# A two-layer trunk with a product-key expert layer: prompt tile first, its expert slots beside the latent front

## The reference

```python
h = rmsnorm(x, g_attn_norm) * (1 + sc1) + sh1
cq, ckv, krope, zb, qc, kc, vc, gates = split(h @ w_in)
oa = attention over low-rank q / kv, 8 heads of 96          # mixer A
ob = gelu(zb)[:512] * (w_s applied per 128-token chunk)     # mixer B
oc = windowed attention, 8 query heads on 2 key heads of 64 # mixer C
x += g1 * ((s(g0)*(oa@w_o_a) + s(g1)*(ob@w_o_b) + s(g2)*(oc@w_o_c)) @ w_out)
h = rmsnorm(x, g_ffn_norm) * (1 + sc2) + sh2
q = h @ w_pq                                   # 8 heads, 2 halves of 128
top 16 of 128 keys in each half, then top 16 of the 256 sums -> 16 experts a head
x += g2 * sum_k gate_k * gelu(u_k . h) * v_k   # 8 x 16 = 128 experts a token
```

## Time and profile before

| | |
|---|---|
| median of 3 runs | 5146.21 us (5142.45 to 5149.38) |
| span of the profiled execution | 5145.4 us, 0.8 us under the median |
| TensorE busy | 3978.3 us (77%) |
| VectorE busy | 2905.9 us (56%) |
| ScalarE busy | 1635.7 us (32%) |
| GpSimd busy | 1556.1 us (30%) |
| bytes moved by DMA | 1640.19 MB, of which 1342.26 MB by the gathers; 319 GB/s over the span |
| mean granted TensorE clock | 0.853 of full speed |

### The profile page before, as it was taken

How to read it: one execution, slowest core, us unless ns; L and a number is a source line. 1 busy time by engine, 2 the same in 40 slices (tenths; PEclk the granted TensorE clock), 3 DMA queues, 4 the chain that set the end, 5 groups by cost and what they waited for, 6 DMA issues and landing times.

```text
span 5145.4 us, 62465 instructions
## 1 busy us (share of the span) xinstructions
PE 3978.3 (77%) x20366; PEld 1626.3 (32%) x20366; DVE 2905.9 (56%) x6315; ACT 1635.7 (32%) x4867; POOL 1556.1 (30%) x1453
## 2 busy tenths in 40 slices
PE   5988899778887666666679889997788887666666
PEld 3555653332223211111134556533322232111111
DVE  3543544675666676654445434446756667766544
ACT  0211542223333333333322115422233333333333
POOL 0210012233334444343312100132333344444432
PEclk8989999988999977666779899998889998677666
DMA  7126049899999999999941260498899999999998
GB/s 281 48 78 236 7 167 399 344 339 372 421 406 409 420 421 421 421 421 421 421 183 48 99 221 1 179 398 340 341 373 421 411 409 413 421 421 421 421 421 357
DMA packets 232449, 1640.19 MB, mean 319 GB/s; under 512 B 26688, under 2 KB 28864, under 8 KB 36800
## 3 DMA queue, kind: packets, MB, share of 16 engines
q0 software_dynamic: 184320, 1342.26, 63.8%
q1 hardware_dynamic: 47808, 293.94, 15.0%
HBM read 1632.82 MB, written 3.28 MB: 318 GB/s over the span
## 4 chain that ended last, share of the span: by engine, by line
PE 37%; DMA 35%; DVE 17%; issue 5%; ACT 4%; DVEq 2%; POOL 1%; SPq 0%; ACTq 0%; POOLq 0%
DMA arena<-in_experts,arena 30%; PE ps L751 12%; PE ps L985 8%; DVE sq L1455 6%; DMA front<-in_experts,arena 3%; PE ps L936 3%; PE ps L961 3%; DMA arena<-in_weights 2%; PE ps L888 2%; PE ps L949 2%; PE ps L913 2%; PE ps L900 1%; ACT arena L1122 1%; DVE arena L1185 1%; DVE negm L1346 1%
## 5 line engine op out<-in xcount | busy, mean ns | idle before, releaser
L985 PE MATMUL ps<-arena 64*64 64x512 f32 x9040 | 1569.3, 777 | 828.2 <-ACT arena L1122 813.5
L724 POOL DMA_INDIRECT arena<-in_experts,arena x1130 | 1261.1, 1116 | 2774.9 <-PE ps L985 1891.6
L1455 DVE CUSTOM_DVE_ANT_0 sq<-arena 128x1024 f32<-128x1024 f32 x1130 | 1386.1, 1227 | 909.4 <-DMA arena<-in_experts,arena 831.3
L985 PEld LDWEIGHTS ps<-arena 64*64 64x64 f32 x9040 | 312.8, 156 | 1923.1 <-issue 1900.5
L1116 ACT ACTIVATE arena<-arena 128x1 f32<-128x1 f32 x1280 | 258.4, 202 | 2073.9 <-DVE arena L1455 2058.2
L751 PE MATMUL ps<-arena 128*128 128x512 f32 (+3 forms) x1920 | 819.3, 574 | 21.9 <-DMA arena<-in_weights 20.0
L1122 ACT ACTIVATE arena<-ident,arena 128x128 f32<-128x128 f32 x1280 | 513.9, 402 | 91.8 <-issue 3.4
L751 PEld LDWEIGHTS ps<-arena 128*128 128x128 f32 x1920 | 360.3, 195 | 467.5 <-issue 427.0
L1118 ACT ACTIVATE arena<-arena 128x1 f32<-128x1 f32 x1280 | 376.7, 294 | 92.1 <-issue 5.2
L961 PE MATMUL ps<-arena 128*128 128x256 f32 (+1 forms) x1536 | 349.3, 372 | 6.3 <-issue 2.3
L961 PEld LDWEIGHTS ps<-arena 128*128 128x128 f32 x1536 | 251.7, 199 | 183.4 <-issue 150.5
(11 more groups left out here) (159 smaller groups left out, 3039.4 us busy)
## 6 DMA issues: line engine op xcount, KB each, us to landing
arena<-in_weights SPq DMA_DIRECT2D x242, 1024.0 KB
arena<-in_experts,arena POOLq DMA_INDIRECT x1130
arena<-mod_rows SPq DMA_DIRECT2D x24, 512.0 KB, 7.1
arena<-in_weights SPq DMA_DIRECT2D x8, 576.0 KB
arena<-in_keysT SPq DMA_DIRECT2D x4, 1024.0 KB, 12.9
arena<-in_g_norm SPq DMA_DIRECT2D x6, 512.0 KB, 9.4
arena<-in_weights SPq DMA_DIRECT2D x4, 768.0 KB
arena<-in_weights SPq DMA_DIRECT2D x6, 512.0 KB
```

The lines of the kernel that those rows point to most:

```text
L724: pool.indirect_dma_start(out=ring[BUF[n]], out_offset=None, in_=ins["experts"], in_offset=bass.IndirectOffsetOnAxis(ap=index(t)[:, slot:s ...
L985: last = MM(acc[h][to:to + 64, c * 512:(c + 1) * 512], diag[n % 4][lo:lo + 64, lo:lo + 64], ring[BUF[n]][lo:lo + 64, D + c * 512:D + (c + ...
L1455: V.tensor_tensor_reduce(out=sq[:], in0=ring[BUF[n]][:, 0:D], in1=h2_of_slot(n), scale=1.0, scalar=0.0, op0=ALU.mult, op1=ALU.add, accum_o ...
```

## The change

The list is written in another order. The prompt runs through inputs, attention, merge, route and choose alone. Its 128 slots are then spread through the whole front of the latent tiles (inputs, attention, merge and route of tile 1). The 512 latent slots follow, with merge and route of tile 2 and then of tiles 3 and 4 spread in, and in layer 0 also the modulation products and the whole prompt front of layer 1. There are now four groups for merge and route, and the input weights are loaded twice a layer (once for the prompt, once for the latents).

```diff
-GROUPS = {0: (0,), 1: (1, 2), 2: (3, 4)}
+GROUPS = {0: (0,), 1: (1,), 2: (2,), 3: (3, 4)}
...
+def prompt(l):
+    norms = first_norms(l, (0,))
...
+    s = norms + inputs_of(l, (0,)) + attention(l, (0,))
+    s += [("rows2", l, 0), ("keys", l, 0)] + merge(l, 0) + route(l, 0, 0)
+    return s
+
+def sample(l):
+    s = first_norms(l, SAMPLE) + inputs_of(l, SAMPLE) + attention(l, SAMPLE)
+    s += [("rows2", l, 1), ("again", l), ("keys", l, 1)] + merge(l, 1) + route(l, 1, 1)
+    return s
...
 def schedule():
-    s = [("start",), ("consts", 0)] + mod_items(0, (0, 1))
+    s = [("start",), ("consts", 0)] + mod_items(0, (0, 1)) + prompt(0) + [("g2", 0, 0)]
     for l in range(L):
...
-        s += attention(l, (1, 2, 3, 4), choose(l, 0)) + [("rows2", l, 1), ("keys", l, 1), ("g2", l, 0)]
         line = Line()
-        line.slots(l)
-        line.spread(-3, 118, pieces(merge(l, 1) + route(l, 1, 1)))
-        line.spread(140, 236, choose(l, 2))
-        line.spread(118, 320, pieces(merge(l, 2) + route(l, 2)))
-        line.spread(322, 372, choose(l, 3))
+        line.slots(l, (0,))
+        line.spread(-1, 134, pieces(sample(l)))
+        s += line.items() + [("g2", l, 1)]
+        line = Line()
+        line.slots(l, SAMPLE)
+        line.spread(-2, 96, pieces(merge(l, 2) + route(l, 2, 2)))
+        line.spread(96, 236, pieces(merge(l, 3) + route(l, 3, 3)))
+        line.spread(240, 300, choose(l, 4))
         if l == 0:
-            line.spread(400, 630, mod_items(1))
-        line.spread(390, 490, choose(l, 4))
+            line.spread(238, 320, [("consts", 1)] + mod_items(1))
+            line.spread(320, 500, pieces(prompt(1)))
```

```diff
-NBUF = 11
-RELEASE = {6: lambda l: ("pq", l, 1, 15), 7: lambda l: ("pq", l, 2, 15), 8: lambda l: ("o", l, NT - 1, 1),
-           9: lambda l: ("sc", l, 2, 15), 10: lambda l: ("n2", l, NT - 1)}
+NBUF = 9
+ALWAYS = 3
+RELEASE = {3: lambda l: ("sw", l, 0), 4: lambda l: ("om", l, NT - 1, 1), 5: lambda l: ("om", l, NT - 1, 1),
+           6: lambda l: ("pq", l, 2, 15), 7: lambda l: ("pq", l, 3, 15), 8: lambda l: ("tk1", l, 3, 15, 1)}
+RETIRE = {3: lambda l: ("hT1", l + 1, 0), 4: lambda l: ("Emm", SLOTS * NT * (l + 1) - 8), 5: lambda l: ("Emm", SLOTS * NT * (l + 1) - 8)}
...
-                elif item[0] == "qT" and item[2:] == (0, 0):
-
-                    l = item[1]
-                    for n in range(l * NT * SLOTS, (l + 1) * NT * SLOTS):
+                elif item[0] == "G":
+                    n = item[1]
...
-        acc = [ps[:, 2 * h:2 * h + 2, :].rearrange("p a n -> p (a n)") for h in range(2)]
+        acc = [ps[:, h, :] for h in range(2)]
...
-                            last = MM(acc[h][to:to + 64, c * 512:(c + 1) * 512], diag[n % 4][lo:lo + 64, lo:lo + 64],
+                            last = MM(acc[h][to:to + 64, :], diag[n % 4][lo:lo + 64, lo:lo + 64],
...
     elif _k == "O":
         if _it[4] == 1:
-            _take(_it, _it[3], 1)
+            _take(_it, 2 + _it[3], 1)
+            _open.add(2 + _it[3])
     elif _k in PAIR:
-        _take(_it, min((4, 6) if _open else (2, 4, 6), key=lambda b: max(_used[b:b + 2])), 2)
+        _take(_it, min((b for b in (2, 4, 6) if not _open & {b, b + 1}), key=lambda b: max(_used[b:b + 2])), 2)
     elif _k in ONE:
-        _take(_it, min(range(4, 8) if _open else range(2), key=lambda b: _used[b]), 1)
+        _take(_it, min((b for b in range(2, 8) if b not in _open), key=lambda b: _used[b]), 1)
```

More of the change, by code:

```diff
@@ L60 @@
 TILES = (0, 1, 2, 3, 4)
+SAMPLE = (1, 2, 3, 4)
 CTX = (5, 6)
@@ new lines @@
+GATHER_AFTER = {}
+_free = {b: -1 for b in range(ALWAYS)}
+_in = {b: (None, 0) for b in range(NBUF)}
+_at = -1
+for _n in range(NSLOT):
+    _l, _s = divmod(_n, NT * SLOTS)
+    _t = _s // SLOTS
+    if _s == 0:
+        for _b in RELEASE:
+            _free[_b] = AT[RELEASE[_b](_l)]
+    _ok = [b for b in _free if b not in RETIRE or AT[("Emm", _n)] < AT.get(RETIRE[b](_l), len(BASE))]
+    _b = min(_ok, key=lambda b: _free[b])
+    _at = max(_at, _free[_b], AT[("tk2", _l, _t, _s % SLOTS // 32, 5)])
+    assert _at < AT[("E", _n)], (_n, _b)
+    GATHER_AFTER.setdefault(_at, []).append(_n)
+    _free[_b] = AT[("Emm", _n)]
+    BUF.append(_b)
+    SAME[_n] = _in[_b][0]
+    TURN_OF[_n] = _in[_b][1] + 1
+    _in[_b] = (_n, TURN_OF[_n])
```

539 lines of the change are left out of this document (281 added, 258 removed).

## The result

The changed kernel took 5410.98 us as the median of 4 runs (5399.06 to 5419.69), the kernel before 5147.8 us on the same chip (5142.45 to 5152.48): a ratio of 1.0507, 95% interval 1.0494 to 1.052. The forecast was 5215 us, at most 5375. The direction was right, the loss four times as large as forecast (263 us against 67). The span of the profiled execution, 5397.2 us, is 181 us over the 5216 of the sum.

| stage | forecast | measured | off |
|---|---|---|---|
| A, prompt alone | 387 | 387.3 | 0 |
| B, layer 0: norms and inputs | 268 | 287.2 | +19 |
| latent attention (slots 48 to 97) | 330 | 360.8 | +31 |
| merge of tile 1 / route and choose | 120 / 114 | 130.0 / 112.7 | +10 / -1 |
| B, layer 1: the same four | 268, 330, 120, 114 | 288.1, 366.9, 130.5, 112.1 | +20, +37, +11, -2 |

The account below looks back on a forecast made before the run. It took TensorE to bound the fronts, DMA the slot stages from 7 buffers on, and VectorE to limit route with 6. Terms 387 + 832 + 1674 + 832 + 1491 = 5216 gave a forecast of 5215 us, range 5030 to 5375.

Parts of the forecast that it names:

- A: Prompt alone through inputs, attention, merge, route and choose, up to the first slot: 387 us.
- B: Prompt slots beside the latent front, once in each layer: 832 us each.
- D: The latent slots of layer 1: 1491 us.
- C: The 512 latent slots of layer 0, including the prompt front of layer 1: 1674 us.
- the term of the latent attention in B: 64 units with 47 slots: 17 units at 3.6 us, 47 at 5.5 us of ScalarE, plus 10: 330 us.
- the ring: Rival: first 97 prompt slots have three circulating buffers and stall if gathers land after over 8.4 us; 5375 to 5533, chance 0.12.
- The attention's own upper bound, 395: Latent attention in B if every slot's 3.64 us of ScalarE came on top in series: 395 us.
- Inputs: Latent norms and inputs in B, with 45 slots in the inputs and TensorE full there: 268 us.
- Merge: Merge of tile 1 in B with 17 slots, 110 us of DMA plus waits at its start: 120 us.
- The turn: The last 12 slots of C and the turn to the next layer: 26 us.
- The prompt front in C: 180 slots beside the prompt front of layer 1, counted by DMA bytes, its attention's table loads covered: 575 us.
- the attention hides it: Rival: table loads fall into TensorE's 207 us, so the latent attention takes 258 and B 760: 5071 us, chance 0.23.

Follow-up runs that it names:

- slot_tanh: The changed kernel with the slot's Gelu replaced by a Tanh, which shares a table set with the Exp: 5266.62 us (one run).
- no_slots_in_attention: The changed kernel with no slots beside the 64 units of latent attention; 43 prompt slots of a layer run later: 5522.93 us, ratio 1.073.
- late_with_free_pairs: Control (changed kernel, all prompt slots behind the latent attention, 5632.61 us) with the values' product moved to banks 0 and 1: 5432.39 us (one run each).
- freed_and_tanh: The changed kernel with no bank held through a mixer, and the Gelu of slots inside an attention made from Square, Tanh and Identity: 5165.48 us, ratio 1.003.

## Why the forecast was wrong

A was right to 1 us, and not by luck: the inputs ended near 150 us, the attention at 190 and the merge at 289, where its terms put 152, 192 and 290. D was right to 10, C's first three parts to 11. One of these holds a slip: 75 slots and 22 blocks are 242 us at 2.49, not 248, so slots 226 to 364 should have stood at 456, against 469 measured.

The step that failed is the term of the latent attention in B, the largest of the misses with 31 and 37 us: "17 units without a slot at 3.6, and 47 where ScalarE does Exp 1.09, copy 0.80 and 3.64". I had taken the tie of scores to the Exp just before as an addition to ScalarE's load, at 3.5 us a unit, which I read from one round of the kernel before at full clock, and let the slot's work and the loads stand in its place. They are two causes. The closed bank pair alone takes 280 us for 64 units, 4.4 a unit, since the round of 3.6 is joined by waits at the ends of mixers and the clock falls (0.84); the loads come on top with 60, and the slots' other work with 6 and 3 (slot_tanh against no_slots_in_attention). The table loads themselves, which I argued at length, were sized well: 94 x 1.3 = 122 us of ScalarE forecast, 119 measured for 89 loads, half of it on the path. In this order of the runs 286 + 6 + 60 is the measured 352 from the first to the last Exp; the stage by its slots is 9 longer. From the other end it is 254 us for the stage with neither cause, against the bound of 258 in the prediction, and 107 for the two, where the prediction had put 72 on top.

The count that should have warned was in my hands: 32 of 64 scores bound instead of 10. I let a tied unit cost 3.6 us against 207 / 64 = 3.2 of the stage before, 0.4 more; late_with_free_pairs against its control gives 93 / 64 = 1.45 over all units, tied or not. The count alone gives no price either, as the 21 bound scores of freed_and_tanh show: it matters what TensorE has to do in the meantime.

The upper end of the range, 5375, came from the ring alone, and the ring's bytes are worth 20 us in both layers together. The attention's own upper bound, 395, was wide enough (65 us a layer above 330, 5346 in the sum), but I left out that the other terms would lean the same way. Without the 68 us of the attention, or without the 58 of the end of C, the time would have been under 5375; it took both. Inputs +19 and +20: half the ring, the rest not tried apart. Merge +10 and +11: not tried. The turn +20: 2 found, the rest open. The prompt front in C +38: 15 a late row, and 17 the table loads, which I had called covered because 35 slots "give it 110 us". The row shows why a stretch that is bound by bytes doesn't cover such a wait: while VectorE stood for it no buffer came free, the stretch moved 381 GB/s instead of 420, and the bytes weren't made up later.

The rival *the attention hides it* would have needed both causes gone. freed_and_tanh has them gone, with 254 us for what it put at 258. It takes 5165 us and not the rival's 5071, since the misses in inputs, merge and C stay. So, as far as that kernel shows it, the trade of the change (idle DMA in the fronts against 88.6 MB of weights) came out at +0.3%, and its two side effects cost 4.8%. The direction was right because the attention holds up the change, on which the forecast rested too: without its 72 us a layer the sum is 5071.

## What to carry to other kernels

Before work is overlapped with a stage, count what it holds there, not only what it executes: here two accumulator banks, closed for the whole program, cost the attention 92 us and more a layer with no slot in it, and about 50 with 47 slots in it. Size a tie by running or reading the whole stage with it, since waits also lower the clock of the matmuls between them. Two functions of different table sets that are interleaved on ScalarE want a form of one in the set of the other, and only where they meet: in all slots the longer form took back most of what it gave. Batches of slots between batches of units were not tried.

## What the runs showed of the hardware

TensorE's granted clock changes level inside one attention. Two windows of the changed kernel, the first behind a wait of TensorE of 1.4 us (ended at 705 us), the second behind waits of 1.6 and 2.8 us (ended at 716 and 723 us). The granted clock was 1.00 from 698 to 725 us and 0.50 from there to 739:

```profile
706.00:712.00 6.00, 5.50 (x51) 3.69 (x50) 2.25 (x4) 4.92 (x8) 1.62 (x1) 1.00 0.28 75
726.00:733.00 7.00, 5.53 (x32) 3.08 (x31) 2.09 (x5) 5.15 (x9) 0.94 (x1) 0.50 0.35 116
```

At 1.00 (2.4 GHz) a slot's eight matmuls take 1.09 us, at 0.50 (1.2 GHz) 1.98. The 64 units of attention, the same instructions, are 178 us of TensorE at a mean of 0.98 and 219 at 0.84. And a table load of 1.28 us cost less than that in time, 0.7, on a ScalarE that is busy for three quarters of the stage. A part of the loads falls into waits: the one at 702.50 us above ends at 703.78, and the maximum for which its Exp waits only at 704.02.
